# Weight sums of a seven-product matrix scheme: made by accumulating DMAs in place of GpSimd tensor operations

## The reference, cut to what matters

```
first block:   h = rms_norm(x);  f = (silu(h @ w_ffn_gate) * (h @ w_ffn_up)) @ w_ffn_down
second block:  h = rms_norm(x) @ w_up_2        # 1024 x 5632
               h = causal convolution of width 3 over the tokens, plus bias
               a, g = split(h);  y = (silu(g) * a) @ w_down_2
```

## Time and profile before

| | us |
|---|---|
| median of 3 runs | 3207.19 |
| the runs | 3198.75, 3207.19, 3208.09 |
| span of the profiled execution, first to last instruction | 3197.4 |
| PE busy | 3000.9 (94%) |
| DVE busy | 1954.1 (61%) |
| ACT busy | 1224.8 (38%) |
| POOL busy | 606.6 (19%) |

### The profile page before, as it was taken

One profiled execution on the slowest core, in us unless ns is written; L12 is line 12 of the kernel. 1 busy time (PEld: TensorE's weight loads), 2 busy tenths in 40 slices (PEclk: granted clock), 3 DMA queues, 4 the chain that ended last, 5 costly groups with the idle time before them and its releaser, 6 DMA issues.

```text
span 3197.4 us, 40840 instructions
## 1 busy us (share of the span) xinstructions
PE 3000.9 (94%) x15215; PEld 2446.6 (77%) x15215; DVE 1954.1 (61%) x2600; ACT 1224.8 (38%) x1900; POOL 606.6 (19%) x533
## 2 busy tenths in 40 slices
PE   8999999999989898999999988999888899999997
PEld 7777878878867677888878877888777677777886
DVE  3555565674674547555556674555646777776667
ACT  3531541531632445333322133565734443333212
POOL 3210110210221301322210000333411222221000
PEclk8999999999989899999999999999989999999999
DMA  4232212212222542222232244343334122223233
GB/s 138 69 94 59 89 60 67 94 54 73 82 80 77 213 145 86 79 79 79 79 113 105 93 131 123 86 135 122 120 106 146 53 79 79 79 72 105 93 105 119
DMA packets 227118, 308.16 MB, mean 96 GB/s; under 512 B 12162, under 2 KB 175248, under 8 KB 224416
## 3 DMA queue, kind: packets, MB, share of 16 engines
q1 hardware_dynamic: 207648, 244.93, 24.1%
q0 software_dynamic: 13520, 44.48, 4.1%
q10 hardware_dynamic: 5808, 16.79, 1.9%
HBM read 223.26 MB, written 82.90 MB: 96 GB/s over the span
## 4 chain that ended last, share of the span: by engine, by line
PE 66%; issue 12%; DVE 9%; ACT 4%; DMA 4%; POOL 4%; SPq 0%; POOLq 0%; ACTq 0%; DVEq 0%
PE PS L658 20%; PE PS L364 19%; PE PS L2314 13%; PE PS L1442 2%; PE PS L1408 1%; PE PS L1336 1%; POOL down_raw L1979 1%; POOL down_raw L1982 1%; PE PS L1325 1%; PE PS L2919 1%; DMA sb_branch<-u_scratch 1%; POOL down_raw L1977 1%; PE PS L2906 1%; DVE hL L439 1%; PE PS L1501 1%
## 5 line engine op out<-in xcount | busy, mean ns | idle before, releaser
L658 PE MATMUL PS<-hH,w_H 128*128 128x512 f32 x1072 | 455.8, 425 | 28.2 <-DVE w_L L321 15.3
L658 PE MATMUL PS<-hH,w_L 128*128 128x512 f32 x1072 | 428.2, 399 | 0.0
L658 PE MATMUL PS<-hL,w_H 128*128 128x512 f32 x1072 | 425.9, 397 | 0.0
L2133 DVE TENSOR_TENSOR ffn_sum<-ffn_sum,PS 128x1024 f32<-128x1024 f32 x160 | 195.4, 1221 | 139.4 <-PE PS L364 139.4
L321 DVE TENSOR_TENSOR w_L<-w_raw,w_H 128x1024 fp32r<-128x1024 f32 x107 | 133.6, 1251 | 217.4 <-ACT w_H L316 217.4
L658 PEld LDWEIGHTS PS<-hH,w_H 128*128 128x128 f32 x1072 | 208.0, 194 | 74.0 <-issue 16.0
L658 PEld LDWEIGHTS PS<-hH,w_L 128*128 128x128 f32 x1072 | 205.8, 192 | 46.8
L2314 PE MATMUL PS<-hH,fast_w 128*128 128x512 f32 x672 | 227.2, 399 | 10.3 <-ACT gate_up L2068 7.6
L658 PEld LDWEIGHTS PS<-hL,w_H 128*128 128x128 f32 x1072 | 207.7, 194 | 35.9 <-issue 1.7
L2212 DVE TENSOR_TENSOR gate_up<-PS,gate_up 128x512 f32<-128x512 f32 x210 | 144.1, 686 | 133.8 <-PE PS L2314 128.7
L2314 PE MATMUL PS<-sums,w_H 128*128 128x512 f32 x672 | 213.9, 400 | 9.3 <-DVE gate_up L2212 8.8
(11 more groups left out here) (459 smaller groups left out, 6569.1 us busy)
## 6 DMA issues: line engine op xcount, KB each, us to landing
w_raw<-in_w_in SPq DMA_DIRECT2D x62, 512.0 KB, 4.4
u_scratch<-unit_staged SPq DMA_DIRECT2D x50, 512.5 KB, 4.9
w_raw<-in_w_up SPq DMA_DIRECT2D x44, 512.0 KB, 4.2
hidden_scratch<-hidden SPq DMA_DIRECT2D x42, 512.0 KB, 3.0
gate_up<-hidden_scratch SPq DMA_DIRECT2D x20, 1024.0 KB, 4.9
w_raw<-in_w_ffn_gate SPq DMA_DIRECT2D x22, 512.0 KB, 3.9
w_raw<-in_w_ffn_up SPq DMA_DIRECT2D x22, 512.0 KB, 5.2
u_scratch<-unit_staged_f SPq DMA_DIRECT2D x21, 512.0 KB, 4.3
```

Of the source, the lines that this page charges most:

```text
L658: mm = e.matmul(PS[:, f.bank(o, half), :], w[:, k0 + k, :], x[:, k, half * HALF:(half + 1) * HALF], start=(k == 0 and j == 0), stop=(k == ...
L2133: e.tensor_tensor(yacc[:, b, :], yacc[:, b, :], bank2(4 + 2 * (b % 2)), ALU.add).then_inc(added, 1)
```

## The change

POOL makes no sum any more. SP loads the second operand of each sum straight into its place: U0 into T1 and T3, U4 into T2, G4 into T4 (four DMAs of 256 KB, `sum_parts`), beside the whole gate tile and the upper half of the up tile into `w_raw` (512 KB and 256 KB, `weights`). Then POOL issues four accumulating DMAs inside SBUF, 256 KB each: T1 += G0 and T3 += U4 together, when both have landed T2 += T1, and when that has landed T4 += T2. The signs of the token sums and of the sums out of PSUM are turned so that every weight sum is an addition. T1 to T4 stand for the same four steps as before: T2 needs T1, T4 needs T2. `T_DONE` says after how many of the four DMAs a sum may be read: T1 and T3 after two, T2 after three, T4 after four. The sixth product (q = 5) goes to a bank of its own, number 3, so that PE waits at q = 5 and q = 1 for earlier sums than before.

```diff
-                ("fast_loaded", "EH", 32 * NW + 16 * NG), ("fast_T", "EH", 4 * NW),
+                ("fast_loaded", "EH", 96 * NW + 16 * NG), ("fast_T", "EH", 64 * NW),
...
-            e.tensor_tensor(s1, s1, x2, ALU.add).then_inc(s, 1)
+            e.tensor_tensor(s1, s1, x2, ALU.subtract).then_inc(s, 1)
...
-        Q_BANK, Q_FIRST = (0, 1, 0, 1, 2, 1, 2), (0, 1, 4)
+        Q_BANK, Q_FIRST = (0, 1, 0, 1, 2, 3, 2), (0, 1, 4, 5)
...
+        T_DONE = (None, 2, 3, 2, 4)
...
+            def weights(j, it=None):
+                e.dma_start(rg[:, :, :], tile(w_first, c_first, j, it)).then_inc(sem("fast_loaded"), 16)
+                e.dma_start(ru[:, 4:8, :], tile(w_second, c_second, j, it)[:, 4:8, :]).then_inc(sem("fast_loaded"), 16)
+
+            def sum_parts(j, it=None):
+
+                for n, (w, col, k0) in ((1, (w_second, c_second, 0)), (3, (w_second, c_second, 0)),
+                                        (2, (w_second, c_second, 4)), (4, (w_first, c_first, 4))):
+                    e.dma_start(t_of(n), tile(w, col, j, it)[:, k0:k0 + 4, :]).then_inc(sem("fast_loaded"), 16)
...
                     e.wait_ge(sem("fast_L"), own("fast_L", tag, 7, it, 7))
                     e.sem_inc(s_held, 1)
-                    for i, (w, col) in enumerate(((w_first, c_first), (w_second, c_second))):
-                        e.dma_start(raw[(U0 + i) % 2][:, :, :], tile(w, col, 2, it)).then_inc(sem("fast_loaded"), 16)
+                    sum_parts(2, it)
+                    weights(2, it)
...
             def weight_sums(c, it):
-                e.wait_ge(sem("fast_loaded"), own("fast_loaded", tag, c * 32 + 32, it, 32))
-                done = lambda n: e.wait_ge(sem("fast_T"), own("fast_T", tag, 4 * c + n, it, 4))
-                e.tensor_tensor(t_of(1), ru[:, 0:4, :], rg[:, 0:4, :], ALU.subtract).then_inc(sem("fast_T"), 1)
-                done(1)
-                e.tensor_tensor(t_of(2), ru[:, 4:8, :], t_of(1), ALU.subtract).then_inc(sem("fast_T"), 1)
-                e.tensor_tensor(t_of(3), ru[:, 4:8, :], ru[:, 0:4, :], ALU.subtract).then_inc(sem("fast_T"), 1)
+                done = lambda n: e.wait_ge(sem("fast_T"), own("fast_T", tag, 64 * c + 16 * n, it, 64))
+                add = lambda n, other: e.dma_start(t_row(n), other, accum_op=ALU.add).then_inc(sem("fast_T"), 16)
+                e.wait_ge(sem("fast_loaded"), own("fast_loaded", tag, c * 96 + 96, it, 96))
+                e.sem_inc(s_held, 1)
+                add(1, rg[:, 0:4, :].rearrange("p k c -> p (k c)"))
+                add(3, ru[:, 4:8, :].rearrange("p k c -> p (k c)"))
                 done(2)
-                e.tensor_tensor(t_of(4), rg[:, 4:8, :], t_of(2), ALU.subtract).then_inc(sem("fast_T"), 1)
+                e.sem_inc(s_held, 1)
+                add(2, t_row(1))
+                done(3)
+                e.sem_inc(s_held, 1)
+                add(4, t_row(2))
...
                 if Q_T[q]:
-                    e.wait_ge(sem("fast_T"), own("fast_T", tag, 4 * c + Q_T[q], it, 4))
+                    e.wait_ge(sem("fast_T"), own("fast_T", tag, 64 * c + 16 * T_DONE[Q_T[q]], it, 64))
...
-                tile_sum(it, 5, uq[:, hi], 2, uq[:, hi], 2)
+                tile_sum(it, 5, uq[:, hi], 2, gq[:, hi], "sub", 2)
...
-                tile_sum(it, 6, gq[:, hi], 1, gq[:, hi], 2)
+                tile_sum(it, 6, gq[:, hi], 3, gq[:, hi], "add", 3)
...
                     if q == 1 and not first:
-                        e.wait_ge(sem("fast_sum"), own("fast_sum", tag, -1, it, 5))
+                        e.wait_ge(sem("fast_sum"), own("fast_sum", tag, -3, it, 5))
...
-                    if q >= 5:
-                        e.wait_ge(sem("fast_sum"), own("fast_sum", tag, q - 3, it, 5))
+                    if q == 5 and not first:
+                        e.wait_ge(sem("fast_sum"), own("fast_sum", tag, -1, it, 5))
+                    if q == 6:
+                        e.wait_ge(sem("fast_sum"), own("fast_sum", tag, 3, it, 5))
```

More of the change, by code:

```diff
@@ L1920, in sp_ffn @@
             load_unit(e, U0 + 1, tile(w_second, c_second, 0))
-            for i, (w, col) in enumerate(((w_first, c_first), (w_second, c_second))):
+            rg, ru = raw[U0 % 2], raw[(U0 + 1) % 2]
+            def weights(j, it=None):
[5 more added lines that the diff above has]
+                    e.dma_start(t_of(n), tile(w, col, j, it)[:, k0:k0 + 4, :]).then_inc(sem("fast_loaded"), 16)
+            for i in range(2):
                 e.wait_ge(s_wH, U0 + 1 + i)
                 e.wait_ge(s_wL, U0 + 1 + i)
-                e.sem_inc(s_held, 1)
-                e.dma_start(raw[(U0 + i) % 2][:, :, :], tile(w, col, 1)).then_inc(sem("fast_loaded"), 16)
+            e.sem_inc(s_held, 1)
+            weights(1)
             ffn_memory_free(e, prev)
+            sum_parts(1)
             e.dma_start(down_first[:, :, :], w_down[:, 0:2, :]).then_inc(sem("down_loaded"), 16)
@@ L2012, in high @@
                 if Q_T[q]:
[L2013 removed]
+                    e.wait_ge(sem("fast_T"), own("fast_T", tag, 64 * c + 16 * T_DONE[Q_T[q]], it, 64))
                 else:
[L2015 removed]
+                    e.wait_ge(sem("fast_loaded"), own("fast_loaded", tag, 96 * c + 96, it, 96))
                 if c or it is not None:
@@ L2106, in turn @@
                     down_high(0, down_first[:, :, :])
-                    e.wait_ge(sem("fast_loaded"), since(tag, "fast_loaded", 32 * NW + 16))
+                    e.wait_ge(sem("fast_loaded"), since(tag, "fast_loaded", 96 * NW + 16))
                     e.activation(hdH[:, 1, :], hidden_first[:, 1, :], ACT.Copy).then_inc(sem("hidden_H"), 1)
@@ L2118, in act_ffn @@
                 down_high(i, rawD)
-                e.wait_ge(sem("fast_loaded"), since(tag, "fast_loaded", 32 * NW + 16 + 16 * i))
+                e.wait_ge(sem("fast_loaded"), since(tag, "fast_loaded", 96 * NW + 16 + 16 * i))
                 for kt in range(2):
@@ L2206, in tile_hidden, with tile_sum @@
                 e.tensor_tensor(hfE[:, :], hfE[:, :] if conv else uq, siE[:, :], ALU.mult).then_inc(hid, 1)
-            def tile_sum(it, p, out, bank, other, before=None):
+            def tile_sum(it, p, out, bank, other, op, before=None):
                 e.wait_ge(sem("fast_P"), own("fast_P", tag, p, it, 7))
@@ L2211, in tile_sum @@
                     e.wait_ge(sem("fast_sum"), own("fast_sum", tag, before, it, 5))
-                e.tensor_tensor(out, PS[:, bank, :], other, ALU.add).then_inc(sem("fast_sum"), 1)
+                x, y = (other, PS[:, bank, :]) if op == "from" else (PS[:, bank, :], other)
+                e.tensor_tensor(out, x, y, ALU.add if op == "add" else ALU.subtract).then_inc(sem("fast_sum"), 1)
             def turn(it, following):
@@ L2230, in turn @@
                 e.wait_ge(sem("fast_taken"), own("fast_taken", tag, 1, it, 2))
-                tile_sum(it, 2, uq[:, lo], 1, gq[:, hi])
+                tile_sum(it, 2, uq[:, lo], 1, gq[:, hi], "from")
                 if first:
@@ L2238, in turn @@
                     low(0, 1, it)
-                tile_sum(it, 4, uq[:, hi], 1, gq[:, hi])
+                tile_sum(it, 4, gq[:, hi], 1, gq[:, hi], "from", 1)
                 if following:
```

13 lines of the change are left out of this document (7 added, 6 removed).

## The result

| | before | after |
|---|---|---|
| median of 4 runs beside each other, us | 3202.97 | 3532.14 |
| runs, us | 3191.45 to 3208.09 | 3531.51 to 3533.60 |
| span of the profiled execution, us | 3197.4 | 3529.7 |
| period of a turn of E / H, us | 19.34 / 20.97 | 27.62 / 28.89 |
| load issue to high(0), E / H, mean us | 5.76 / 5.71 | 9.18 / 8.98 |

After takes 1.1045 times as long (95% interval 1.1017 to 1.1073). The spans differ by 332.3 us. Over 19 periods between POOL's marks, E's turn is 8.28 us longer and H's 7.92; 20 such turns in each are 166 + 158 = 324 us. The last 8 us lie around them; the runs of the kernel before spread over 17 us among themselves. I forecast 3385, with a range of 3280 to 3500: direction and loop came out, the price of the accumulating DMAs did not.

A forecast was written before the change was run, and what follows sets the result against it. H was bound by the loop from load through T2 to low(6), E by PE, with 1.74 us slack. H's 5.45 and E's 3.7 us more per turn made 183 us: 3380, plus 5 gave 3385; range 3280 to 3500.

The forecast's parts named there:

- POOL's operations go, DVE gains: DVE's low parts run faster without POOL working: 0.85 us a turn gained in E, 1.45 in H.
- Loads: 768 KB more per turn: 2.6 us more in both phases, plus 0.6 in H for meeting the store.
- Accumulating DMAs: Between loads and high(1): the pair, then T2, take 6.6 us instead of 3.0, 3.7 more with the semaphore's way.
- dear: Rival: accumulations cost 7.3 us more than now, 3.6 a turn above the sum, giving 3530; chance 0.25 for above 3440.
- Bank 3, signs: PE's earlier waits are not on the loop and turned signs keep the instruction count: zero.
- The first turn: At each phase's start, loads wait for the preceding phase's buffers, but there is room: zero, at most 3 us each.
- The clock: Half clock at q = 6 after PE's gap: hidden in H, at most 0.9 us a turn in E, 18 us.
- The sum: Turns of 26.4 us in H and 23.05 in E, 183 us more over 20 turns each.
- The loop: H's turn is a loop from load to low(6) and back; what is added before T2 returns every turn.
- the rival of the other side: DVE's gain outweighs the costs: H's loop falls to 19.52 us, 29 us less, 3175; chance 0.03.

The follow-up runs named there:

- e3: The changed kernel with its four DMAs inside SBUF as plain copies, no addition: 3420.69 us, 1.0704 of before.
- e6: The kernel before with only the turned signs, bank 3 and PE's earlier waits: 3197.62 us, 1.0005 of before.
- e5: The changed kernel with 44 transposes keeping PE busy ahead of q = 6: 3515.69 us, 1.1006 of before.
- e1: The changed kernel with its loads kept, but the four additions made by GpSimd tensor operations again: 3310.92 us, 1.0354 of before.
- e7: The kernel before with 768 KB of its loads issued early, only 256 KB behind low(6): 3198.54 us, 1.0000 of before.
- e10: The kernel before with early loads and H's second up tap cut to 64 columns: 3174.31 us, 0.9940; with the short tap alone 3197.02 us.
- e8: The changed kernel with its loads split and issued early, still with accumulating DMAs: 3301.04 us, 1.0337 of before.

## Why the prediction was wrong, by its own steps

**POOL's operations go, DVE gains: right.** low(1) and low(2) are at 0.69 us in both phases, as written.

**Loads: nearly right.** Forecast 2.6 more in E and 3.2 in H, measured 3.42 and 3.27, inside the bounds. In E, where the store stood behind the loads before too, as much came on top of the transfer's 2.6 us as in H, so the 0.6 us that I put down to the store may be something else, such as SP's four additional issues: the six took 5.0 us in H (2696.80 to 2701.83) where I had 3. No run separates them, so that H's sum came out is partly luck. E: 0.8 x 20 = 16 us of the miss, H: 1.

**Accumulating DMAs: this step failed.** I counted one as its bytes doubled at the rate I read off two stores of the earlier trace rows, 32 KB in 2.1 us and 512 KB in 2.9. That gave 6.6 us for the pair and T2 in place of 3.0, 3.7 more with the semaphore's way. Measured is high(0) to high(1) at 9.45 in place of 3.15, 6.3 more. Of the 2.6 us a turn that are missing (by the turn of H shown above, whose 9.3 us lie a little below the mean):

- About 1.0 is POOL's start. T1's DMA starts 0.58 us after high(0) where the operation started at 0.04, and POOL takes 0.50 us again between the pair's landing and T2's issue (the "issue" rows of the chain above). I had put 0.1 for all of this.
- About 1.1 is the pair. From its issue to its landing pass 0.45 + 4.28 us and a little, 4.8, where I had 3.7. In it, each issue costs POOL 0.85 us, not 0.54, and 512 KB move at 180 to 190 GB/s.
- About 0.4 is T2, 3.25 to its landing and 3.36 to high(1), where I had 2.9.

So two terms were wrong. The slope: 480 KB in 0.8 us is 600 GB/s, taken from DMAs that do not add, and doubled bytes made 300 of it, where some 190 was real. And the start: each link of the chain costs POOL half a microsecond before it issues. The range's upper end for this step (7.3 more) held; the 6.3 lies nearer to it than to my 3.7. This is 2.6 us in 40 turns, 104 us. The rival "dear" put 144 us on top of my sum by the accumulations alone and so met the time (3530) by luck: by the terms below, its 144 are 104 of these, 17 of loads and 23 of the clock.

Both estimates from the Trainium skill can now be placed. "DMA: Bandwidth & Descriptors" (section "Anatomy of one DMA — SWDGE (gpsimd) path"), 5.8 us for pair and T2, describes e3's plain copies (3.68 + 2.3 = 6.0), not accumulations. The other page of the Trainium skill, "Collectives: The Full Stack" (Part 3, on the bandwidth ceiling), half the rate where an addition needs two reads per write (the page says it of ReduceScatter), gave 3.2 us for a single one, and 3.2 is its landing; for the pair it gave 4.4, and 4.3 is the landing by the page of the profile. After's 180 and 193 GB/s are 0.51 and 0.55 of e3's 350, so this trace agrees with half the rate; what both estimates lack is POOL's 0.5 us before each issue. Had I gone by that rule, the sum would have been 36 us higher, and this step would have missed by 68 us in place of 104.

**Bank 3, signs: right.** e6 shows both. **The first turn:** its first DMA is issued 3.0 us later than T1 began before in E (1237.24 against 1234.22), the bound I gave. It is a part of the 8 us around the turns, which no run divides.

**The clock: left out, and wrongly so.** I had 0.9 us a turn of E "at most", in the range only. By e5 it is 27.62 - 26.49 = 1.13 us a turn. The gap itself, forecast at 4 us, was 6; and e1 shows that one of 2.56 us was followed by half the clock as well.

**The sum, with measured terms.** H: 20.97 + 3.27 + 6.28 - 1.45 = 29.07 (28.89 measured). E: 17.6 + 3.42 + 6.31 - 0.85 = 26.48, which is e5's 26.49, and with the clock's 1.13 it is 27.61 (27.62). The miss of 149.7 us in the span (3529.7 less 3380): 104 accumulation, 17 loads, 23 clock (1.13 x 20), and some 6 that are not assigned: 8 lie around the turns, and the terms above are 4 too high in H (29.07 for 28.89, 20 times).

**The loop: right for this change, incomplete as a picture.** "So H is a loop" holds for anything added between load and T2. But e7 to e10 show a second loop behind it, of nearly the same length: what is taken out of the first comes back only if the second gives way too. Had the sums become cheaper, the rival of the other side (29 us gained in H) would hardly have come either; no run tests it.

## What to carry to other kernels

Before an operation is handed from an idle engine to DMAs, price the issue, the start, the fixed part and the rate of that kind of DMA, and count them once for every link of a dependent chain; an operation of 1.3 us on an idle engine is cheaper than a DMA that is 3.2 us from issue to landing. A rate read from transfers that do not add is no price for those that do: here it promised 300 GB/s, and they had some 190. An idle stretch that a longer chain makes on PE has a price of its own, the clock after it: in E 23 us. And the slack in a waiting row on one loop is a bound for a gain only until the next loop, which one experiment that cuts both shows.

## What the runs showed of the hardware

- An accumulating DMA inside SBUF, 256 KB on 128 partitions: 3.2 us from issue to landing, two at once 4.3; a plain copy of the same shape 2.3 and 2.6; half the columns 2.6 and 3.0. In full flow 180 and 193 GB/s for what is added, at a DMA share of 1.05 and 1.10; 350 GB/s at 0.91 for the plain copy.
- GpSimd's issue of one is 0.85 us, of a plain copy 0.54, and half the columns cost the same 0.85. Queue q0 has 37712 packets in after and 26960 in e3 with the same 168 DMAs and bytes: 64 packets more for each that adds.
- GpSimd issued a DMA 0.5 us after the landing that it waited for (0.53 and 0.50 in the chain of after), where its tensor operation started 0.04 us after high(0).
- An accumulation beside loads from memory took 5.86 us to the next issue (e8) in place of 3.83.
- The stretch from 1357.0 to 1363.5 us, around the end of a gap of 6.07 us of PE, was granted 0.50 (1.2 GHz); with the gap filled the same stretch was granted 1.00 (2.4 GHz). In e1 a gap of 2.56 us was followed by 0.50 from 1611 to 1613 us.
